# One block for the experts and the last stage, with the expert rows loaded from SyncE's queue

## The reference, cut to what matters

```python
def dispatch_experts(x, expert, weight, w_up, w_gate, w_down):
    # top-2 of 32 experts per token; blocks of 128 rows, one expert each
    ...
    def expert_block(args):
        xi, ei = args
        return (jax.nn.silu(xi @ w_gate[ei]) * (xi @ w_up[ei])) @ w_down[ei]

    yb = lax.map(expert_block, (xb, blk_e)).reshape(n_rows, D_MODEL) * row_w[:, None]
    return jnp.zeros((n_tok + 1, D_MODEL), x.dtype).at[row_tok].add(yb)[:n_tok]

def channel_and_ple(x, p, ...):
    x = x + hier_moe(rmsnorm(x, g_moe), ...)
    gate = jax.nn.sigmoid(rmsnorm(x, g_ple) @ w_pg)
    return x + gate * (p @ w_pp)
# and last: y = rmsnorm(x, g_final)
```

## Time and profile before

| what | value |
|---|---|
| device time, median of 3 runs (lowest to highest) | 1881.11 us (1879.85 to 1882.21) |
| device time of the profiled execution | 1886.54 us |
| its span | 1884.6 us |
| TensorE matmul busy | 1716.0 us (91%) |
| VectorE busy | 1111.8 us (59%) |
| ScalarE busy | 934.7 us (50%) |
| GpSimd busy | 203.0 us (11%) |
| mean granted TensorE clock | 0.956 |

### The profile page before, as it was taken

How to read it: one execution, slowest core, us unless ns; L and a number is a source line. 1 busy time by engine, 2 the same in 40 slices (tenths; PEclk the granted TensorE clock), 3 DMA queues, 4 the chain that set the end, 5 groups by cost and what they waited for, 6 DMA issues and landing times. The chain is left out here.

```text
span 1884.6 us, 27080 instructions
## 1 busy us (share of the span) xinstructions
PE 1716.0 (91%) x9848; PEld 1466.8 (78%) x9848; DVE 1111.8 (59%) x1341; ACT 934.7 (50%) x1344; POOL 203.0 (11%) x294
## 2 busy tenths in 40 slices
PE   6999999989899997899589967999999999998597
PEld 6999999978787776677478755888888888887376
DVE  5111222145277766332465375999999999997466
ACT  5221111111365662436343136778787787876255
POOL 1000111130000000300000021311111111110100
PEclk9999999989999998899699978999999999998799
DMA  5443455455362203312665157999999999995542
GB/s 190 130 135 113 129 171 164 135 165 162 118 192 72 64 35 130 112 54 68 233 208 178 70 189 270 392 379 376 377 378 376 382 375 385 379 374 221 211 165 91
DMA packets 163495, 393.27 MB, mean 209 GB/s; under 512 B 21475, under 2 KB 105043, under 8 KB 142932
## 3 DMA queue, kind: packets, MB, share of 16 engines
q1 hardware_dynamic: 125444, 312.35, 46.7%
q10 hardware_dynamic: 22544, 43.80, 6.3%
q0 software_dynamic: 15424, 36.00, 6.0%
HBM read 335.84 MB, written 80.58 MB: 221 GB/s over the span
## 5 line engine op out<-in xcount | busy, mean ns | idle before, releaser
L2667 DVE TENSOR_TENSOR x_wgl<-x_wg,x_wgh 128x2048 fp32r<-128x2048 f32 x66 | 148.3, 2288 | 37.1 <-ACT x_wgh L2604 19.6
L2667 DVE TENSOR_TENSOR x_wul<-x_wu,x_wuh 128x2048 fp32r<-128x2048 f32 x66 | 148.2, 2288 | 18.4 <-ACT x_wuh L2604 18.4
L97 PE MATMUL p_acc<-uh,p_wl 128*128 128x344 f32 x480 | 156.9, 327 | 0.0
L2689 DVE TENSOR_TENSOR x_wdl<-u,x_wdh 128x1024 fp32r<-128x1024 f32 x128 | 148.2, 1220 | 11.5 <-ACT x_wdh L2610 11.5
L99 PE MATMUL p_acc<-uh,p_wh 128*128 128x344 f32 x480 | 153.8, 320 | 0.0
L98 PE MATMUL p_acc<-ul,p_wh 128*128 128x344 f32 x480 | 153.8, 320 | 0.0
L463 DVE COPY u<-p_turn 128x512 f32<-128x512 f32 x40 | 25.8, 686 | 185.2 <-PE p_turn L284 185.1
L2610 ACT ACTIVATE x_wdh<-u 128x1024 fp32r<-128x1024 f32 x128 | 124.9, 1059 | 0.0
L2604 ACT ACTIVATE x_wgh<-x_wg 128x2048 fp32r<-128x2048 f32 x64 | 119.1, 1915 | 0.6 <-DMA x_wg<-in_w_pg 0.6
L2604 ACT ACTIVATE x_wuh<-x_wu 128x2048 fp32r<-128x2048 f32 x64 | 118.6, 1906 | 0.0
L390 ACT ACTIVATE p_zc<-p_acc 128x344 f32<-128x344 f32 x60 | 27.3, 458 | 178.5 <-PE p_acc L99 174.7
(11 more groups left out here) (422 smaller groups left out, 4496.5 us busy)
## 6 DMA issues: line engine op xcount, KB each, us to landing
x_wg<-in_w_gate SPq DMA_DIRECT2D x64, 1024.0 KB, 7.4
x_wu<-in_w_up SPq DMA_DIRECT2D x64, 1024.0 KB, 7.7
u<-in_w_down SPq DMA_DIRECT2D x32, 2048.0 KB, 12.5
zT<-p_zc ACTq DMA_DIRECT2D x30, 516.0 KB, 3.4
p_w<-in_w_in SPq DMA_DIRECT2D x30, 512.0 KB, 5.4
ztok<-u POOLq DMA_DIRECT2D x20, 512.0 KB, 4.6
f_y<-ys POOLq DMA_DIRECT2D x16, 512.0 KB, 5.4
u<-in_x_prompt SPq DMA_DIRECT2D x13, 512.0 KB, 7.7
```

The source lines that it names most:

```text
L97: pe.matmul(out, w_low, m_high, start=first, stop=False)
L2667: dve.tensor_tensor(wl[:, s, :], w[:, s, :], wh[:, s, :], ALU.subtract).then_inc(full, 1)
L2689: dve.tensor_tensor(wdl[:, k, :], wd[:, b, k, :], wdh[:, k, :], ALU.subtract).then_inc(dl_full, 1)
```

## The change

`experts` and `finish` become one function with one block, so nothing stands between the two on any engine. The last stage's instructions on TensorE, ScalarE and VectorE follow the tails of `experts` in the same streams, in the same order as before. To have both in memory at once, the last stage's buffers are laid over those of the experts: `y2` over `x_wdh`, the two `pps` buffers over `x_xh` and `x_xl`, `uTh` and `uTl` over `x_wdl`, `gf` over the first two parts of a joined `hidden` tile (before: `gs`, `sg`, `hm` apart), `tp` over `tpx`, the gate products over `Y`, and `gate8` over a joined `G`/`U` tile.

POOL has nothing left to do in the last stage. SyncE issues everything, in one list that follows its `w_pg` loads. `rows_landed` is gone; SyncE waits for `x_y_out` itself.

```diff
-def experts(nc, g):
+def experts_and_finish(nc, g, y_of):
...
+        hidden_parts = sb("hidden", [P, 3, FE])
+        gs, sg, hm = (hidden_parts[:, n, :] for n in range(3))
...
+        both_ps = ps("GU", [P, 2, FE])
+        G, U_ = (both_ps[:, n, :] for n in range(2))
...
+        gf = hidden_parts[:, 0:2, :].rearrange("p x n -> p (x n)")
+        y2 = wdh[:, :, :].rearrange("p k n -> p (k n)").bitcast(F32).rearrange("p (t c n) -> p t c n", t=2, c=2)
...
+        pps = [t[:, :, :].rearrange("p k n -> p (k n)").bitcast(F32) for t in (xh, xl)]
...
+            def last_rows(np_):
+                sp.dma_start(gp[:, :], ...).then_inc(gp_in, 16)
...
+                def load_y(t):
+                    need(sp, mix, 2 * (t - 1))
+                    for c in range(2):
+                        sp.dma_start(y2[0:rows(at(t)), t % 2, c, :], ys[c * NT + at(t) * P:c * NT + at(t) * P + rows(at(t)), :])\
+                            .then_inc(y_in[t % 2], 16)
+
+                load_h(0)
+                sp.wait_ge(u_full, np_ * 2)
+                load_pps(0)
+                load_pps(1)
+                sp.wait_ge(dl_full, np_ * (2 * KF) - KF)
+                load_h(1)
+                sp.wait_ge(hm_full, np_ * 2)
+                sp.dma_start(gf[:, :], g["g_final"].unsqueeze(0).broadcast_to([P, D])).then_inc(gf_in, 16)
+                sp.wait_ge(dl_full, np_ * (2 * KF))
+                load_h(2)
+                for b in range(2):
+                    sp.wait_ge(g["x_y_out"][b], np_ * 16)
+                for t in range(3):
+                    load_y(t)
+                for t in range(3, TT):
+                    load_h(t)
+                load_y(3)
+                for v in range(TT):
+                    sp.wait_ge(yo_full, v + 1)
+                    sp.dma_start(y_of(at(v)), yo[0:rows(at(v)), v % 2, :]).then_inc(sent[v % 2], 16)
+                    if v + 2 < TT:
+                        load_pps(v + 2)
+                    if v + 4 < TT:
+                        load_y(v + 4)
...
-def finish(nc, g, y_of):
...
-        @block.gpsimd
-        def _(pool):
...
-                pool.wait_ge(g["x_y_out"][b], np_ * 16)
-                pool.sem_inc(rows_landed, 1)
-            pool.wait_ge(rows_landed, 2)
-            for t in range(TT):
-                need(pool, mix, 2 * (t - 1))
-                for c in range(2):
-                    pool.dma_start(y2[0:rows(at(t)), t % 2, c, :], ys[...])\
-                        .then_inc(y_in[t % 2], 16)
```

More of the change, by code:

```diff
@@ L2590, in _, with turn_row, decode_half, gated_half @@
             passes(pe, step, end)
+            def turn_row(t):
+                r = rows(at(t))
+                pe.wait_ge(mix, 2 * t + 2)
+                need(pe, uT_full, t)
+                by_k = h[:, at(t), :].rearrange("t (p k) -> t k p", k=KD)
+                for k in range(KD):
+                    last = pe.transpose(tp[:, k, 0:r], by_k[0:r, k, :], ident[0:r, 0:r])
+                last.then_inc(tp_full, 1)
+            def decode_half(c):
+                cols = slice(c * C, (c + 1) * C)
+                if c == 0:
+                    pe.wait_ge(uT_full, 1)
+                for kk in range(KD // QUADS):
+                    for j in range(QUADS):
+                        k = j * (KD // QUADS) + kk
+                        last = pe.matmul(gate8[j * QUAD:j * QUAD + DEC, cols], uT8[:, k, :], raw[c][:, k, :],
+                                         start=(kk == 0), stop=(kk == KD // QUADS - 1), skip_group_check=True,
+                                         tile_position=(0, j * QUAD))
+                last.then_inc(gate_full, 1)
+            def gated_half(v, c):
+                r = rows(at(v))
+                cols = slice(c * C, (c + 1) * C)
+                if v >= 2:
+                    pe.wait_ge(sig_full, (v - 1) * 2 + c + 1)
+                pe.wait_ge(uTl_full, v)
+                for k in range(KD):
+                    last = products(pe, gate_ps[c][0:r, :], uTh[:, v % 2, k, 0:r], uTl[:, v % 2, k, 0:r],
+                                    wpgh[c][:, k, :], wpgl[c][:, k, :], k == 0, k == KD - 1)
+                last.then_inc(gate_full, 1)
+            turn_row(0)
+            turn_row(1)
+            for c in range(2):
+                decode_half(c)
+            for v in range(1, TT):
+                gated_half(v, 0)
+                if v + 1 < TT:
+                    turn_row(v + 1)
+                gated_half(v, 1)
         @block.scalar
@@ L2655, in _, with square, norm_root @@
             passes(act, step, end)
+            def square(t):
+                r = rows(at(t))
+                act.wait_ge(mix, 2 * t + 2)
+                need(act, ssq, t)
+                need(act, ssq2, t - 3)
+                act.activation(sq[0:r, :], h[0:r, at(t), :], ACT.Square, accum_out=st[0:r, 0, t:t + 1]).then_inc(ssq, 1)
+            def norm_root(t):
+                r = rows(at(t))
+                act.wait_ge(mean, t + 1)
+                act.activation(st[0:r, 1, t:t + 1], st[0:r, 1, t:t + 1], ACT.Sqrt).then_inc(root, 1)
@@ new lines, in last_square @@
+            def last_square(v):
+                r = rows(at(v))
+                if v < TT - 1:
+                    act.wait_ge(h_full, 2 * v + 2)
+                    act.wait_ge(ssq, min(TT, v + 4))
+                    need(act, ssq2, v)
+                    act.activation(sq[0:r, :], h[0:r, at(v), :], ACT.Square, accum_out=st[0:r, 3, v:v + 1]).then_inc(ssq2, 1)
+                else:
+                    act.activation(st[0:r, 1, v:v + 1], st[0:r, 1, v:v + 1], ACT.Sqrt)
+                    for c in range(2):
+                        act.wait_ge(h_full, 2 * v + 2 * c + 2)
+                        act.activation(sq[0:r, c * C:(c + 1) * C], h[0:r, at(v), c * C:(c + 1) * C], ACT.Square,
+                                       accum_out=st[0:r, 3 + 3 * c, v:v + 1]).then_inc(ssq2, 1)
@@ new lines, in last_root @@
+            def last_root(v):
+                r = rows(at(v))
+                act.wait_ge(mean2, v + 1)
+                act.activation(st[0:r, 4, v:v + 1], st[0:r, 4, v:v + 1], ACT.Sqrt).then_inc(root2, 1)
+            square(0)
+            square(1)
+            high_parts(1)
+            norm_root(0)
+            norm_root(1)
+            act.wait_ge(gate_full, 2)
+            act.activation(near8, gate8[0:DEC, :], ACT.Copy).then_inc(quads, 1)
+            square(2)
+            norm_root(2)
@@ new lines, in _ @@
+            act.wait_ge(inv, 1)
+            act.wait_ge(quads, QUADS)
+            act.activation(sig[0:DEC, 0, :], near8, ACT.Sigmoid, scale=st[0:DEC, 2, 0:1]).then_inc(sig_full, 2)
+            for v in range(1, TT - 1):
+                gate_out(v, 0)
+                high_parts(v + 1)
+                if v + 2 < TT:
+                    square(v + 2)
+                gate_out(v, 1)
+                last_square(v - 1)
+                if v + 2 < TT:
+                    norm_root(v + 2)
+                last_root(v - 1)
@@ L2657, in _ @@
+            last_square(TT - 2)
+            last_root(TT - 2)
+            for c in range(2):
+                gate_out(TT - 1, c)
+            last_square(TT - 1)
+            last_root(TT - 1)
         @block.vector
@@ L2994, in low_parts, with gated_row @@
                     .then_inc(uTl_full, 1)
-            def gated(v):
+            def gated_row(v):
                 r = rows(at(v))
@@ L3002, in gated @@
                 dve.wait_ge(pps_in[v % 2], 16 * (v // 2 + 1))
[L3003 to L3004 removed]
+                need(dve, sent[v % 2], 16 * (v // 2))
+                dve.tensor_tensor(yo[0:r, v % 2, :], sig[0:r, v % 2, :], pps[v % 2][0:r, :], ALU.mult)\
                     .then_inc(h_full, 1)
@@ L3060, in _ @@
                     mixed(v + 2)
-                gated(v - 1)
+                gated_row(v - 1)
                 if v + 2 < TT:
@@ L3068, in _, with gather, scatter, step @@
             for v in range(TT - 2, TT):
-                gated(v)
+                gated_row(v)
                 last_mean(v)
                 last_norm(v)
+        @block.gpsimd
+        def _(pool):
+            def gather(n, b, it):
+                need(pool, tpx_full, it * 2 + (b - 1))
+                pool.tensor_copy(idx[:, 0, b:b + 1], from_token[:, bass.ds(n, 1)]).then_inc(idx_full, 1)
+                pool.wait_ge(idx_full, n + 1)
+                pool.sem_inc(gather_due, 1)
+                pool.indirect_dma_start(x[:, b, :], None, xs[0:NT, :],
+                                        bass.IndirectOffsetOnAxis(ap=idx[:, 0, b:b + 1], axis=0), bounds_check=NT - 1, oob_is_err=False)\
+                    .then_inc(x_in[b], 16)
+            def scatter(n, b, it):
+                need(pool, y_out[b], it * 16)
+                pool.tensor_copy(idx[:, 1, b:b + 1], to_row[:, bass.ds(n, 1)]).then_inc(row_full, 1)
+                pool.wait_ge(row_full, n + 1)
+                pool.wait_ge(y_read, n * 2 + 2)
+                pool.sem_inc(scatter_due, 1)
```

(15 more changed lines are left out.)

235 lines of the change are left out of this document (52 added, 183 removed).

## The result

The changed kernel took 1894.75 us (median of 4 runs, 1891.96 to 1896.19) beside 1880.48 us (1879.81 to 1882.21). The ratio is 1.0073, with a 95% interval of 1.0055 to 1.009: slower by 14.3 us, where 9.2 us was forecast and 1882 to 1899 us was the range. A second series beside other experiments gave 1893.08 against 1880.44 us, 12.6 us.

What follows compares the result with a forecast made beforehand. A VectorE-ScalarE chain with a load at its front was taken to set the end. Terms of -7.5, -2.5, +18.2 and +1 summed to +9.2 us on the 1881.1 us median: 1890.3 us, range 1882 to 1899 us.

Steps and rivals of the forecast that it cites:

- seam: Stretch from the last matmul and scatter to the last stage's first tile; forecast to shorten by 7.5 us.
- five stands: VectorE's waits for `y` rows at `mixed(4)` to `mixed(8)`: 2.6 us, then four of 3.9, together +18.2 us.
- clock in the last tile: TensorE's clock falling after the last wait, slowing the last tile's matmuls on the end path; +1 us.
- Part 1: Between scatter and `mixed(0)`: SyncE's first load follows the scatter's landing at once; -7.5 us, bounds -8.2 and -6.
- cover: Early loads issued under the experts' tail, costed at nothing; without this they would delay `y(0)` by 2.3 us.
- Part 2: At `mixed(2)`: `y(2)` goes out ahead of the `h` loads, so VectorE's wait for it goes; -2.5 us.
- Part 3: In the passes: `y(v+4)` queues behind `yo_full`, store and `pps`, so VectorE waits in five passes; +18.2 us.
- Part 4: TensorE's clock halves after gaps of about 3.5 us, hidden in the passes but not the last tile; +1 us.
- A: Rival for the passes: VectorE's existing idle time absorbs the wait for `y`; faster, 1871.6 us, chance 9%.
- B: Rival for the passes: the four transfers overlap, waits of 2.1 to 2.9 us; 1880.3 to 1884.3 us, chance 12%.
- C: Rival for the passes: TensorE's clock falls and stays low during the waits; 1904 to 1919 us, chance 6%.

Runs made afterwards that it cites:

- h_at_seam: Changed kernel with `y(v+4)` issued before the `yo_full` wait, and `h(0)`, `h(1)`, `pps(0)` issued between the scatter's landing and `y(0)`; 1877.08 us, ratio 0.9973.
- two_blocks_ahead: Kernel before, both blocks kept, with `y` loads moved to SyncE and `y(v+4)` issued before the `yo_full` wait; 1881.31 us, ratio 0.9994.
- after_again: The changed kernel run once more, unaltered; 1893.08 us, ratio 1.0068 to the kernel before.
- y_first: Changed kernel with the `y` loads issued ahead of the store and `pps` load, still behind the `yo_full` wait; 1885.63 us, ratio 1.0018.
- pps_early: Changed kernel with `pps(v+2)` issued before the `yo_full` wait, once `gated(v)` has read its buffer; 1885.99 us, ratio 1.0026.
- two_blocks_sp: Kernel before, both blocks and own buffers kept, with only the `y` loads moved to SyncE in the changed kernel's order; 1903.25 us, ratio 1.0116.

## Why the prediction was right

The direction, the place and the mechanism came out as stated, and the time lies in the range, 4.5 us above the forecast's 1890.3. By its own steps, from the scatter's issue, the profile accounts for 12.2 of the 14.3 us; the rest is under "What stays open":

| step | forecast | first profile after |
|---|---|---|
| seam, at the start of `mixed(1)` | -7.5 | -7.3 |
| `mixed(2)` | -2.5 | -2.3 |
| five stands, to the start of `mixed(8)` | +18.2 | +20.2 |
| clock in the last tile | +1 | +1.6 |
| sum | +9.2 | +12.2 |

**Part 1** held. SyncE's load goes out as soon as the scatter has landed. Its cover, costed at 2.3 us, measured 3.6 in h_at_seam, which changes nothing in the sum as long as the cover is there.

**Part 2** held: without the seam, in two_blocks_ahead, the reordered `y(2)` is worth only 1.5 us, because the `h` loads are still late there.

**Part 3** is the term that decided, and it was sized 2.0 us too low. Most of that is in two places. For `y(4)` a store of 32 KB was taken to save a whole transfer (stand 2.6 us); it saved 0.7 at most, and the stand was 3.26 us (3.65 in after_again, 0.35 less than the next). And the last stands grew to 4.2 and 4.6 us (4.1 and 4.5 in after_again); why they grow isn't known. The stands sum to 19.8 us; the other 0.4 is that each pass is also 0.08 us longer apart from its stand. Serial transfers at 401 GB/s fit only roughly, as y_first showed. By the Trainium skill's 2.0 us plus bytes (DMA: Bandwidth & Descriptors, "Anatomy of one DMA"), a fit that the page gives for loads issued by GpSimd, an estimate of the stand would be 3.5 us; measured were 3.8 to 4.6 for the full ones, so the rows were the better guide. The Trainium skill's sentence that another issuer saves only issue time (the same page, "Issuing engines are not separate DMA queues") fits two_blocks_ahead, where SyncE in place of POOL changed nothing in the passes (12.9 us).

**Part 4** had the size but not the condition. I took a gap of some 3.5 us to bring the clock down, as in the earlier trace rows. TensorE's gap ahead of the first product was 2.85 us in both profiles of the changed kernel; in one the clock fell in all five such gaps, in the other in none of four. In pps_early it fell 0.7 us behind the end of a gap of 2.18 us, shorter than the 2.57 us without a fall. The gap alone doesn't decide it, and so the term was 1.6 us in one execution and 0 in the other. The low clock also ended sooner in the passes, after about 3.5 us and not 6.8.

**The rivals.** A (the loop swallows the stand) is refuted: each us of wait lengthened its pass. B (the transfers overlap) is refuted in its size: the full stands are 3.8 to 4.6 us and not 2.1 to 2.9 (the upper end of its sum is 2.8 by its own terms). In its mechanism it may hold in part, by y_first. C (the clock stays low) did not occur.

**What stays open.** The medians differ by 14.3 and 12.6 us, the profiles' parts from the scatter on by 12.2 and 11.3. Where the remaining 1 to 2 us lie is not shown. They can't be put down to the joined block: in all eleven other profiles the median, set against the kernel before of its series, stands 0.3 to 2.7 us higher than the profiles' parts say, and two_blocks_sp and two_blocks_ahead, which keep both blocks, are the two ends (21.5 against 18.9, and -1.2 against -1.5). The kernel before has one profile only, of an execution 5.4 us above its median; a last part 1 to 2 us longer than usual in it would give such a difference everywhere. A cost ahead of the seam would have to be in all eleven, two of which leave the experts' block as it was. In the twelve profiles the part ahead of the scatter lasted from 1739.1 to 1745.9 us, in the kernel before the longest of all; I can't tell a cost of the change there from this spread.

## What to carry to other kernels

When loads move into another engine's instruction list, write down for each the event it stood behind before and the one it stands behind now. SyncE issued its list in order (in the changed kernel the `y` loads went out 0.9 us after the store, 1796.03 against 1795.17), so a load whose buffer is free still waits for the event that the store ahead of it waits for. If that store closes a pass whose successor needs the load, most of the transfer is exposed in every pass: 7.5 us from the store's issue, 3.4 of them covered. A joined block can be kept and its gain won by asking for the rows one pass earlier, here one moved line: 1873 us in place of 1893 to 1895.

## What the runs showed of the hardware

Four 512 KB transfers issued back to back by SyncE, a store and three loads, had the reader of the last start 7.3 to 8.1 us after the first issue; with one load less it was 5.8 to 6.3 us (pps_early). In y_first, with two loads ahead and a store and a load behind, the reader started 5.8 us after the first issue, and 5.5 us where the store behind had 32 KB.

In the same kernel, at the same gap of 2.85 us, the granted TensorE clock fell to 0.50 in all five gaps of one execution and in none of the four of another. The shortest such gap with a fall close behind it was 2.18 us (pps_early), and one of 2.57 us had none. A low clock of about 3.5 us per pass cost no time in the passes, where TensorE had over 4 us to spare, and 1.6 us in the last tile.

The end of one block of five engine streams and the opening of the next took 4.3 us between the last scatter's issue and the first reader (13.63 us in two_blocks_ahead, 9.38 in h_at_seam, with the same loads ahead of it but for one of 4 KB).
